# Two transformer blocks and a mixture of experts on one core: where a norm's inverse root is applied, and what the first units of a projection wait for

## The reference: what is computed

```
def rms_norm(x, g):
    xf = x.astype(jnp.float32)
    y = xf * lax.rsqrt(jnp.mean(xf * xf, axis=-1, keepdims=True) + RMS_EPS)
    return (y * g.astype(jnp.float32)).astype(x.dtype)
def swiglu_ffn(x, w_in, w_out):
    gate, up = jnp.split(x @ w_in, 2, axis=-1)
    return (jax.nn.silu(gate) * up) @ w_out
...
        h = h + rms_norm(mixed, mix_norm_post[layer])
        normed = rms_norm(h, ffn_norm_pre[layer])
        h = h + rms_norm(swiglu_ffn(normed, ffn_w_in[layer], ffn_w_out[layer]), ffn_norm_post[layer])
```

## Time and profile before

| | |
|---|---|
| runs | 2242.27, 2245.85, 2246.39 us |
| median | 2245.85 us |
| profiled execution | 2246.82 us, of it 2245.0 us span |
| busy share of the span | PE 76%, weight loads 53%, DVE 30%, ACT 26%, POOL 6% |
| chain that ended last | PE 51%, DMA 38%, DVE 5%, ACT 3%, POOL 1%, issue 1% |
| mean granted TensorE clock | 0.879 of full speed |
| read from HBM | 594.71 MB |

### The profile page before, as it was taken

How to read it: one execution, slowest core, us unless ns; L and a number is a source line. 1 busy time by engine, 2 the same in 40 slices (tenths; PEclk the granted TensorE clock), 3 DMA queues, 4 the chain that set the end, 5 groups by cost and what they waited for, 6 DMA issues and landing times.

```text
span 2245.0 us, 27132 instructions
## 1 busy us (share of the span) xinstructions
PE 1707.0 (76%) x11760; PEld 1186.1 (53%) x11760; DVE 675.8 (30%) x973; ACT 577.4 (26%) x962; POOL 135.2 (6%) x153
## 2 busy tenths in 40 slices
PE   7998899979888999697888665566565555656655
PEld 7898799968557999595678631111111111111111
DVE  4644454454546444462555310000000000000001
ACT  3354344433654343341554210000000000000000
POOL 1101100010221000100321000000000000000000
PEclk8999899979999999898999788887878787888778
DMA  9843455528582555353126269999999999999995
GB/s 233 271 148 113 159 170 186 187 76 245 215 309 93 182 176 187 112 169 94 57 76 241 116 278 428 427 428 428 428 428 428 427 427 428 429 426 428 429 427 246
DMA packets 160620, 603.54 MB, mean 269 GB/s; under 512 B 9542, under 2 KB 114151, under 8 KB 132711
## 3 DMA queue, kind: packets, MB, share of 16 engines
q1 hardware_dynamic: 147712, 587.23, 66.9%
q10 hardware_dynamic: 12808, 14.85, 3.1%
HBM read 594.71 MB, written 4.19 MB: 267 GB/s over the span
## 4 chain that ended last, share of the span: by engine, by line
PE 51%; DMA 38%; DVE 5%; ACT 3%; POOL 1%; issue 1%; ACTq 0%; DVEq 0%
PE ps L616 20%; DMA late_expert_slots<-in_w_exp_down 13%; DMA late_expert_slots<-in_w_exp_gate 13%; PE ps L653 12%; DMA late_expert_slots<-in_w_exp_up 11%; PE ps L640 3%; PE ps L1133 3%; PE ps L600 2%; DVE split_operands L538 2%; PE ps L995 1%; PE ps L1154 1%; POOL residual L2039 1%; DVE inv_root L1567 1%; PE ps L804 1%; PE ps L983 1%
## 5 line engine op out<-in xcount | busy, mean ns | idle before, releaser
L616 PE MATMUL ps<-split_operands 128*128 128x256 f32 x3744 | 466.1, 287 | 18.8 <-DVE split_operands L561 14.4
L616 PEld LDWEIGHTS ps<-split_operands 128*128 128x128 f32 x3744 | 460.8, 194 | 21.8 <-issue 21.0
L538 DVE TENSOR_TENSOR split_operands<-dense_ring,split_operands 128x1024 fp32r<-128x1024 f32 x288 | 353.4, 1269 | 352.0 <-ACT split_operands L530 352.0
L530 ACT ACTIVATE split_operands<-dense_ring 128x1024 fp32r<-128x1024 f32 x288 | 288.1, 1050 | 286.0 <-PE ps L653 161.1
L2007 DVE TENSOR_TENSOR arena<-arena,ps 128x512 f32<-128x512 f32 x16 | 11.0, 688 | 870.8 <-PE ps L1133 870.8
L1133 PE MATMUL ps<-late_expert_slots,arena 128*32 128x512 f32 x768 | 131.0, 817 | 103.9 <-DMA late_expert_slots<-in_w_exp_gate 53.6
L1133 PE MATMUL ps<-dense_ring,arena 128*32 128x512 f32 x768 | 125.6, 789 | 80.3 <-DMA dense_ring<-in_w_exp_gate 41.9
L653 PE MATMUL ps<-split_operands 128*128 128x256 f32 x1152 | 148.5, 294 | 26.4 <-DVE split_operands L548 17.6
L653 PEld LDWEIGHTS ps<-split_operands 128*128 128x128 f32 x1152 | 147.3, 203 | 28.5 <-issue 15.5
L653 PE MATMUL ps<-hidden_split,split_operands 128*128 128x256 f32 x1056 | 134.4, 289 | 8.4 <-DVE split_operands L538 8.4
L653 PEld LDWEIGHTS ps<-hidden_split,split_operands 128*128 128x128 f32 x1056 | 132.2, 196 | 8.8 <-issue 8.8
(11 more groups left out here) (272 smaller groups left out, 1599.9 us busy)
## 6 DMA issues: line engine op xcount, KB each, us to landing
dense_ring<-in_w_exp_gate SPq DMA_DIRECT2D x24, 2048.0 KB, 36.7
dense_ring<-in_w_exp_up SPq DMA_DIRECT2D x24, 2048.0 KB, 36.1
late_expert_slots<-in_w_exp_up SPq DMA_DIRECT2D x24, 2048.0 KB, 36.7
dense_ring<-in_w_exp_down SPq DMA_DIRECT2D x24, 2048.0 KB, 36.0
late_expert_slots<-in_w_exp_gate SPq DMA_DIRECT2D x24, 2048.0 KB, 35.9
late_expert_slots<-in_w_exp_down SPq DMA_DIRECT2D x24, 2048.0 KB, 36.4
dense_ring<-in_ffn_w_in SPq DMA_DIRECT2D x44, 1024.0 KB, 5.1
dense_ring<-in_ret_w_in SPq DMA_DIRECT2D x24, 1024.0 KB, 11.9
```

What stands on the lines that cost most here:

```text
L530: act.activation(w_hi[:, n % 2, c], ring[U % RING][:, c], ACT.Copy).then_inc(hi_ready, 1)
L538: dve.tensor_tensor(w_lo[:, n % 2, c], ring[U % RING][:, c], w_hi[:, n % 2, c], ALU.subtract).then_inc(lo_ready, 1)
L616: mm = pe.matmul(ps[:, bank, b * T:b * T + T], left, right, start=k == 0 and i == 0, stop=k == 7 and i == 2)
```

## The change

1. **Roots behind the products.** At the four norms ahead of the retention, both networks and the key and value projection, the tokens that are split are stream x gain, without the inverse root (`tokens_hi` on ACT with the gain as scale, `gained_lo` on DVE). The inverse root is the same for all features of a token, so it is multiplied behind the product: into the rotation tables, onto the value copies (turned to one value per partition by `turn_rs`), onto the retention gates (`g_scale`), onto gate and silu of the network (`gate`, `silu_scale`) and onto keys (`kv_out`). Gates now take DVE x rs, ACT silu in place, then DVE x rs again and x up.
2. **First units in step.** `pair_products` multiplies the first two units of such a projection k-step by k-step: chunks 0 to 3 for both, 4 to 7 for the first, then the matmuls of the norm's sum, then 4 to 7 of the second. Both units are split before.
3. **`post`** squares the accumulator bank by bank as the last unit finishes them (`acc_done`), and its residual add moves from POOL to DVE; three DVE operations per chunk, the third being `gained_lo`.
4. **Retention.** Silu of gates in four buffers, RO no longer waits for all four heads (`free` frees its banks one by one).
5. **Bias tables** move from the start into two norms (`bias_table(0)` behind the one of RO, `bias_table(1)` behind the one of FFN 0), their 0.55 MB loads to the end of retention; small loads on the ACT queue move into FFN 0, the mixer's into FFN 1.
6. **Last pair of a network:** its hidden values are split into the token buffers, so that output unit 10 needs not wait until unit 9 is done with the hidden buffers.
7. **Context.** Squares in the NO stage, sum behind it, root and reciprocal in FFN 1, scaling in six POOL operations of 128x1024 in FFN 1; its keys and values are multiplied beside the norm ahead of the mixer. Keys and values of the stream come right after the wide units, ahead of UA and Q (`IN2_ORDER`), and the DMAs into `kd2` are issued in UA. The last query rotation now stands ahead of the first row maximum on DVE.
8. **Merge.** Product b and the sum of both branches go bank by bank on DVE as PB finishes its banks; the last update of the stream goes by banks of WO as well.

```diff
-IN2_ORDER = [4, 5, 6, 7, 0, 1, 2, 3] + list(range(8, 22))
+IN2_ORDER = [4, 5, 6, 7, 12, 13, 0, 1, 2, 3, 8, 9, 10, 11] + list(range(14, 22))
...
+            def pair_products(U, banks, place, x0, between):
+                def chunk(v, k):
+                    hi, lo = parts_of(U + v)
+                    if k % 4 == 0:
+                        pe.wait_ge(lo_ready, 2 * SPLIT_NO[U + v] + k // 4 + 1)
+                    for b in range(2):
+                        for i, (w, x) in enumerate(((hi, x_hi), (hi, x_lo), (lo, x_hi))):
+                            left, right = place(b, w[:, k, :], x[:, k, :])
+                            mm = pe.matmul(ps[:, banks[v], b * T:b * T + T], left, right,
+                                           start=k == 0 and i == 0 and b == 0, stop=k == 7 and i == 2,
+                                           skip_group_check=True)
+                    return mm
+                for k in range(4):
+                    pe.wait_ge(xlo_ready, x0 + k + 1)
+                    chunk(0, k)
+                    chunk(1, k)
+                for k in range(4, 8):
+                    pe.wait_ge(xlo_ready, x0 + k + 1)
+                    mm = chunk(0, k)
+                mm.then_inc(used, 1)
+                between()
+                for k in range(4, 8):
+                    mm = chunk(1, k)
+                mm.then_inc(used, 1)
...
+            pair_products(U_RET, (5, 7), lambda b, w, x: (w[:, b::2], x), X_RET, lambda: norm(N_PRE0))
...
+                    if last and b in (1, 3, 5):
+                        mm.then_inc(acc_done, 1)
...
+            for u in range(8):
+                row_pair(U_RO, u, 8, X_RO, ACC[N_POST0], ((g_sc, 7), None, (g_sc, 8), (oroot, 4)))
+            norm(N_POST0)
             pe.wait_ge(on_ev, 4)
-            for u in range(8):
...
+                pair_products(U0, (gate_bank(f, 0), gate_bank(f, 0) + 1), by_feature, x0, lambda: norm(n))
+                if f == 0:
+                    pe.wait_ge(brow_ev, 1)
+                    pe.wait_ge(cbias_ev, 1)
+                else:
+                    pe.wait_ge(ctx_root, 1)
...
+                pe.wait_ge(xlo_ready, (X_H0, X_H1)[f] + 1)
+                row_T(U0 + 32, [two_chunks(v, 0) for v in (x_hi, x_lo)], acc, False, True)
...
+            def tokens_hi(posted, name):
+                for k in range(DC):
+                    if posted is not None:
+                        act.wait_ge(h_ready, POST[posted] + k + 1)
+                    act.activation(x_hi[:, k, :], h[:, k, :], ACT.Copy, scale=col(name, k)).then_inc(xhi_ready, 1)
+                    if k % 2:
+                        act.activation(sq[:, k - 1:k + 1, :], h[:, k - 1:k + 1, :], ACT.Square).then_inc(sq_ready, 1)
...
+            def gained_lo(x0, name, k):
+                dve.wait_ge(xhi_ready, x0 + k + 1)
+                dve.scalar_tensor_tensor(out=x_lo[:, k, :], in0=h[:, k, :], scalar=col(name, k), in1=x_hi[:, k, :],
+                                         op0=ALU.mult, op1=ALU.subtract).then_inc(xlo_ready, 1)
+            def post(n, name, U, x0=None, next_name=None):
+                split_lo(dve, U)
+                split_lo(dve, U + 1)
+                inverse(n)
+                for k in range(11 if next_name else 9):
+                    if k < 8:
+                        dve.scalar_tensor_tensor(out=xn[:, k, :], in0=acc_chunk(ACC[n], k), scalar=col(name, k),
+                                                 in1=rs[:], op0=ALU.mult, op1=ALU.mult).then_inc(scaled, 1)
+                    if 1 <= k < 9:
+                        dve.wait_ge(scaled, POST[n] + k)
+                        dve.tensor_tensor(h[:, k - 1, :], h[:, k - 1, :], xn[:, k - 1, :],
+                                          ALU.add).then_inc(h_ready, 1)
+                    if next_name and k >= 3:
+                        gained_lo(x0, next_name, k - 3)
...
+            def g_scale(u):
+                taken(dve, U_RET + 16 + u)
+                if u >= 4:
+                    dve.wait_ge(og_done, u - 3)
+                dve.tensor_tensor(gs[u % 4].rearrange("p (c t) -> p c t", c=2),
+                                  ps[:, 5 + 2 * (u % 2), :].rearrange("p (c t) -> p c t", c=2), two(rs[:]),
+                                  ALU.mult).then_inc(g_sc, 1)
...
+                def gate(j, r=0):
+                    taken(dve, gate_unit(f, j), r)
+                    dve.tensor_tensor(halves(f_silu[:, j % 2, :]), halves(ps[:, gate_bank(f, j), :]), two(rs[:]),
+                                      ALU.mult).then_inc(f_gate, 1)
+                def silu_scale(j, r=0):
+                    dve.wait_ge(f_act, r * 2 + (base + j + 1))
+                    dve.tensor_tensor(halves(f_silu[:, j % 2, :]), halves(f_silu[:, j % 2, :]), two(rs[:]),
+                                      ALU.mult).then_inc(f_sc, 1)
...
+            def kv_out(u):
+                taken(dve, U_KV + u)
+                bank = (1, 3, 5, 7)[u]
+                dve.tensor_tensor(kv_raw[:, u], ps[:, bank, :].rearrange("p (t n) -> p t n", t=2), two(rs[:]),
+                                  ALU.mult).then_inc(kv_ev, 1)
...
+            pe.wait_ge(ctx_ready, 2)
+            take(U_K)
+            keys(ctxn, 7).then_inc(kc_mm, 1)
             norm(N_IN2)
+            take(U_V)
+            values(ctxn, 6).then_inc(vc_mm, 1)
             for u in range(4):
                 wide_tok(U_IN2 + u, (2 * (u // 2), 2 * (u // 2) + 1), u % 2, x0=X_IN2 if u < 2 else None)
-            for u in range(4):
-                if u >= 2:
-                    pe.wait_ge(ua_ev, u - 1)
-                col_T(U_IN2 + 4 + u, 5 + 2 * (u % 2))
+            pe.wait_ge(kc_ev, 1)
+            keys(xn, 7).then_inc(used, 1)
+            values(xn, 4).then_inc(used, 1)
...
-            residual(N_POST1)
-            residual(N_POSTF1)
+            pool.wait_ge(gains_set, 1)
+            pool.wait_ge(ctx_inv, 1)
+            for q in range(2):
+                c = ctxn[:, 4 * q:4 * q + 4, :]
+                for i, (v, op) in enumerate(((ctx_rs.unsqueeze(1), ALU.mult),
+                                             (gain[:, 1, 4 * q:4 * q + 4].unsqueeze(2), ALU.mult),
+                                             (mod[:, 1, 4 * q:4 * q + 4].unsqueeze(2), ALU.add))):
+                    if i:
+                        pool.wait_ge(ctx_step, 2 * q + i)
+                    pool.tensor_tensor(c, c, v.to_broadcast([P, 4, T]), op).then_inc(ctx_step if i < 2 else ctx_ready, 1)
...
+            product_b(0)
+            product_b(1)
+            merge(0)
+            product_b(2)
+            merge(1)
+            pair_lo(dve, X_WO, 0, two_chunks(gb, 0))
+            product_b(3)
+            merge(2)
+            merge(3)
```

787 lines of the change are left out of this document (442 added, 345 removed).

## The result

| | before | changed kernel |
|---|---|---|
| median | 2245.99 us (four runs) | 2178.18 us (2174.21 to 2182.02, four runs) |
| ratio to before | | 0.9702, 95% interval 0.9681 to 0.9722 |
| profiled execution | 2246.82 | 2177.85 |

The account below looks back on a forecast made before the run. Up to 1310 us PE's chain of waits was taken to bound the kernel, then a fixed-length stream of experts' weights. Terms summed to -101.8 us from the profiled 2246.82, giving 2145.0 us, range 2134 to 2168.

Parts of the forecast that it names:

- edits at nothing: Edits priced at no cost: network pairs, silu order, load releases, tables' loads on ACT's queue; bias tables 0 to +1 us.
- A: Program start: both units split first, bias tables gone, but rotation waits for root and tables; -0.5 us, bounds -4 and +4.
- H: Mixer, FFN 1's end to window scores: transfers hidden, shorter norm, -33.3 us; later first maximum +4.4 against it.
- J: WO's end to first expert product: last update by bank leaves less ahead of the router's norm; -1.5 us.
- B: RO: its wait for the last head's norm and split goes, and the clock loss behind it; -10.7 us.
- C: Two norms behind RO, to unit 1's end: second sum, root, reciprocal and a chunk pass go under products; -11.9 us.
- E: Norms behind FFN 0, up to the compression: 59.5 us become 49.5; -10.0 us.
- F: Norms behind NO, up to output unit 0 of FFN 1: 48.8 us become 36.1; -12.7 us.
- rival 1: PE's clock stays low behind each norm, costing that much at six places: +12 us, 2157 us; chance 0.14.
- D: Last output unit of FFN 0: with its own buffers its split runs beside unit 9, ending the wait; -7.0 us.
- G: Last output unit of FFN 1: with its own buffers its split runs beside unit 9, ending the wait; -5.9 us.
- Rival 2: Experts' stream was set by its transfers all along, so the end stays at about 2247 us; chance 0.02.

Follow-up runs that it names:

- e1: Changed kernel with the six small loads of FFN 0 issued ahead of the 3 MB bias write instead of behind it; 2146.79 us, ratio 0.9569.
- e8: Changed kernel with five of the six small loads ahead of the 3 MB write and one (192 KB) behind it; 2153.77 us, ratio 0.9593.
- e6: e1 with PB's gated product again behind the whole of PB and the sum of both branches on POOL; 2161.64 us, ratio 0.9628.
- e5: e1 with the first two units of a projection multiplied one after the other instead of in step; 2144.64 us, ratio 0.9553.
- e9: e1 with the program's first two units in turn and unit 2's split ahead of the first root and reciprocal; 2133.66 us, ratio 0.9514.
- e11: e1 plus e9's start, context steps spaced one per pair, e10's unread matmuls, and last query rotation behind head 3's maximum; 2133.69 us, ratio 0.9505.
- e12: e11 with the second gate unit's split on DVE also moved behind the maximum of head 2; 2134.36 us, ratio 0.952.
- e10: e1 plus four unread f32 matmuls on PE ahead of the first products behind FFN 0 and behind NO; 2144.04 us, ratio 0.956.

## Why the prediction was wrong

**The step that failed** is among the edits at nothing: "the tables' loads on ACT's queue sit among idle ACT time". It counts ACT's idle time and does not ask what stands ahead in the same queue. The diff puts the 3 MB write and the six loads into one function, one behind the other; before, 220 us lay between them. The term was put at nothing without a row for it, and cost 30.4 us: ACT's issues stood behind the write, ACT's splits behind the issues, DVE's behind ACT's, and PE waited 27.8 us and lost 2.6 to the clock. Without it, the kernel takes 2146.8 (e1), against 2145.0 foretold; by the ratios to the kernel before, 0.9569 against 0.9550. That this is so close is in part luck: A, H and J gave 7.0 us more than forecast, and the other rows together 9.4 less, the reserve counted. The Trainium skill, page DMA: Bandwidth & Descriptors, section "Issuing engines are not separate DMA queues", calls the time a sequencer needs to initiate a transfer usually small relative to the transfer. Ahead of the write the trace agrees (0.41 us for 192 KB in e1, 3.8 to land); behind it the trace differs (8.10 in the changed kernel, 12.55 in e8).

**The rest, by its terms.** *A*: -2.7 for -0.5, inside its bounds; the steps that it lists add up to 44.6 and not 43.6, which would have made it +0.5. *B*: -10.3 for -10.7; the feared margins of retention cost 0.7 us at one place. *C, E, F*: each 1.2 to 1.7 less than said. The path was right, but the clock is at half for some 4 us in the first products (2.2 us behind RO), and my reserve of 0.5 each was too small; rival 1 had this loss, at 12 us in all against the 4.2 by which these rows missed. It put it behind idling; behind RO and FFN 0 the dip began with PE busy. *D, G*: the wait of output unit 10 went in both (7.0 of row D is there, beside the stall); G lost 2.4 to POOL's context steps, rival 3 in its smallest form (its six steps took 2.4 to 2.9 us each, not 4.4). *H*: 3.0 better; the scores come 109.5 behind FFN 1, said were 112.1, and the maximum's wait is 4.0 for 4.4. *I*: -15.4 for -15.2, shown by e6 (+15.5 when it is taken back). *J*: the last norm gained 1.8 more. What made A, H and J better was not tried.

**Reasons that did not hold though their sum did.** By e5's expectation, in-step products were worth 3.9 to 4.7 us at a norm; e5 shows 0.3 to 0.5. So the gain of C, E and F does not come from the interleaving, which even costs 5.9 us at the start. What is left is the roots behind the products, the single pass over chunks and the sum in the shadow; no run takes these apart.

**Rivals.** Rival 2 fell: the stream begins with PE (1239.5) and is as long as before, 2.2 us more. Rival 4 fell: the pairs of both networks run at 17.28 us. That the time lay above the range came from no rival; the range held bounds of the terms that I had priced, and nothing for an edit priced at zero.

## What to carry to other kernels

Before a small transfer is moved, look at what its queue holds at the new place: behind this write of 2048 pieces and 3 MB the issuing engine stood still, and with it all compute in its order; put short transfers ahead, and the long one last, where the next issue is far away. Price an edit "at nothing" as carefully as the others: name the queue, what is ahead in it and how long that takes to land. And ask of an interleaving what it waits for first: in step, PE gets no further than the first chunk of one unit before the other is split. An effect on the clock needs several executions of both kernels: here one of each pointed to a gain that two other kernels had without the cause.

## What the runs showed that I had not expected

- An issue on ACT's queue took up to 12.6 us behind a transfer that needs 35 us to land, and 0.4 to 0.7 us ahead of it. Before the change, the same write ran from 30 to 65 us with nothing behind it, and cost the queue nothing.
- PE's granted clock was at half in the products that followed the tables' matmuls with hardly any idling (behind RO, in every kernel of the change). Behind 2.2 us of idling (behind NO) it was at half in eight kernels and at 1.0 in e8 and e9, where the same code ran. So a wait of PE can cost more than its length, by 1.5 us here, and need not.
- The same code has two lengths of its sparse attention. In e11's profiled execution (2123.81 us) the clock stayed at 1.0, in e12's (2131.09) it fell for a while, where no line of the two kernels differs:

```profile
552.00:570.00 18.00, 15.22 (x131) 8.42 (x130) 13.52 (x50) 14.80 (x63) 9.03 (x15) 1.00 0.60 224
```

```profile
555.00:573.00 18.00, 15.27 (x106) 8.57 (x106) 12.46 (x47) 11.66 (x52) 8.14 (x13) 0.81 0.47 165
```

From FFN 0's first output unit to FFN 1's, e11 (410.0), e9 (411.9), e10 (411.3) and e8 (412.2 without its 10.8) have the short form, e12 (417.5), e1 (416.4) and e5 (417.1) the long one; e12 has the filler and e8 and e9 have not, so the filler does not decide it. Totals can therefore differ by 5 to 7 us between executions of one kernel, and smaller gains are to be read from stretches, and those against their own spread. e11's five runs lie in two groups, two at 2124 to 2125 and three at 2134. Its profiled execution is in the lower one, 9.5 us below e9's: 2.4 by the context steps, 4.9 in the window attention (the rotation), 1.9 between the two networks, 0.3 elsewhere. That the upper group and e12's runs have the long form would explain the equal medians; only profiled executions can be placed, so this is not shown, and what starts a dip was not tried.
